# Two-block transformer stack on one core: modulation vectors by wide dot products, with the first block's products set among them

## The reference, cut to what matters

```
mod = silu(c) @ w_ada + b_ada            # c: [1, 2048], w_ada: [2048, 6144]
shift, scale, gate = split(mod, 3)       # 2048 values each
u = rms_norm(x, norm_w) * (1 + scale) + shift
proj = u @ w_in                          # w_in: [2048, 19064], cut into 16 parts
...
x = x + gate * (merged @ w_out)
```

## Time and profile before

| | |
|---|---|
| median of 3 runs | 3606.37 us |
| the profiled execution's own time | 3606.82 us |
| its span, of which all rows tell | 3605.0 us |
| TensorE busy, products | 3485.0 us (97%) |
| TensorE busy, weight loads | 2997.6 us (83%) |
| VectorE busy | 2280.1 us (63%) |
| ScalarE busy | 1689.4 us (47%) |
| GpSimd busy | 31.1 us (1%) |
| moved by DMA | 705.67 MB, mean 196 GB/s |

### The profile page before, as it was taken

The page is one execution under the profiler, slowest core; times in us unless marked ns, Lnnn a source line. Parts: engine busy times, 40 slices in busy tenths (PEclk is TensorE's granted clock), DMA queues, the critical chain, the costliest instruction groups (busy, mean ns, idle before and its releaser), DMA issues. The chain is left out here.

```text
span 3605.0 us, 45068 instructions
## 1 busy us (share of the span) xinstructions
PE 3485.0 (97%) x18836; PEld 2997.6 (83%) x18836; DVE 2280.1 (63%) x2722; ACT 1689.4 (47%) x2076; POOL 31.1 (1%) x61
## 2 busy tenths in 40 slices
PE   7999999998999999999999999999999999999998
PEld 7779878877888887799888888888888789988887
DVE  7687666756677456677655576664566676554544
ACT  2354564454333344545644543433445775443333
POOL 0000000000000000000000000000000000000000
PEclk7899999999999999999999999999999999999999
DMA  9654455456667545444444367765555444455554
GB/s 374 231 203 158 152 199 198 175 185 231 257 253 287 200 181 196 163 161 146 162 144 149 124 223 254 256 258 193 187 187 181 167 166 141 153 211 193 191 186 153
DMA packets 99387, 705.67 MB, mean 196 GB/s; under 512 B 11680, under 2 KB 11696, under 8 KB 15600
## 3 DMA queue, kind: packets, MB, share of 16 engines
q1 hardware_dynamic: 93888, 675.38, 51.5%
q0 software_dynamic: 4864, 24.95, 2.0%
q10 hardware_dynamic: 432, 2.45, 0.2%
HBM read 696.45 MB, written 6.29 MB: 195 GB/s over the span
## 5 line engine op out<-in xcount | busy, mean ns | idle before, releaser
L1365 ACT ACTIVATE HH<-RAW 128x2048 fp32r<-128x2048 f32 x546 | 1045.2, 1914 | 1201.5 <-PE G L1107 905.1
L1701 DVE TENSOR_TENSOR LL<-RAW,HH 128x2048 fp32r<-128x2048 f32 x546 | 1248.0, 2287 | 337.2 <-ACT HH L1365 335.8
L1107 PE MATMUL G<-HH,UH 128*128 128x512 f32 x2560 | 1028.0, 402 | 33.2 <-DVE LL L1701 27.6
L1107 PE MATMUL G<-LL,UH 128*128 128x512 f32 x2560 | 1006.4, 393 | 0.0
L1107 PE MATMUL G<-HH,UL 128*128 128x512 f32 x2560 | 1006.0, 393 | 0.0
L1107 PE MATMUL G<-UH,HH 128*128 128x256 f32 x2080 | 605.0, 291 | 14.5 <-DVE LL L1701 8.4
L1107 PEld LDWEIGHTS G<-HH,UH 128*128 128x128 f32 x2560 | 485.9, 190 | 154.2 <-DVE LL L1701 37.4
L1107 PE MATMUL G<-UL,HH 128*128 128x256 f32 x2080 | 590.5, 284 | 0.0
L1107 PE MATMUL G<-UH,LL 128*128 128x256 f32 x2080 | 590.4, 284 | 0.0
L1107 PEld LDWEIGHTS G<-LL,UH 128*128 128x128 f32 x2560 | 485.6, 190 | 104.9
L1107 PEld LDWEIGHTS G<-HH,UL 128*128 128x128 f32 x2560 | 486.4, 190 | 102.2 <-issue 4.1
(11 more groups left out here) (327 smaller groups left out, 2506.9 us busy)
## 6 DMA issues: line engine op xcount, KB each, us to landing
RAW<-in_w_in_packed_dram SPq DMA_DIRECT2D x402, 1024.0 KB, 4.8
RAW<-in_w_ada_packed_dram SPq DMA_DIRECT2D x96, 1024.0 KB, 5.1
RAW<-in_w_out_packed_dram SPq DMA_DIRECT2D x48, 1024.0 KB, 4.8
RAW<-in_w_o_ssd_packed_dram SPq DMA_DIRECT2D x32, 1024.0 KB, 4.8
RAW<-in_w_o_fox_packed_dram SPq DMA_DIRECT2D x16, 1024.0 KB, 4.8
RAW<-in_w_o_dsa_packed_dram SPq DMA_DIRECT2D x16, 1024.0 KB, 5.2
RAW<-in_w_proj_a_packed_dram SPq DMA_DIRECT2D x16, 1024.0 KB, 4.8
RAW<-in_w_proj_b_packed_dram SPq DMA_DIRECT2D x16, 1024.0 KB, 4.8
```

The lines of the kernel that those rows point to most:

```text
L1107: mm = pe.matmul(to, lt, rh, start=first, stop=end, skip_group_check=True)
L1365: a.activation(HH[g % NH][:, :n], RAW[ch["f"] % NR][:, :n], ACT.Copy).then_inc(*hi_done.up(g))
L1701: v.tensor_tensor(LL[f % NR][:, :n], RAW[f % NR][:, :n], HH[g % NH][:, :n].bitcast(F32), ALU.subtract).then_inc(*lo_done.up(g))
```

## The change

All modulation is done as dot products along the row. The host hands w_ada over transposed (`w_ada_turned`), so that an output column lies on a partition and k runs along the row. c is broadcast over the partitions: `CB` (128x2048, silu of it made once by ScalarE and VectorE) for the opening, `CH` (half of it, loaded by POOL's queue from a copy in DRAM) afterwards. One instruction of VectorE with an accumulator gives 128 columns of the result (`dot`, 128x2048), or in the body two such instructions over 1024 values per chunk (`ada_v`). Results lie in `DOT`, ready as columns; only gate is turned into a row, by four products of 128 columns (`fold_pe`). In the opening eight of 32 dots (two of shift in each group, `ON_PE` = 2) are TensorE's, 16 products of one column each.

The opening (`open`) goes through four groups of four column tiles: eight dots and one chunk of the first block in each, then `am_first` and `u` for that group alone. The products of the chunk of group g stand behind the fourth dot (i = 3) of group g + 1. The ring has eight buffers there (`NX` = 3 more, which lie where YH and YL come later), and five after it. The angle tables, which the opening before contained, go into the slots.

```diff
-NR, NH = 5, 3
+NR, NX, NH = 5, 3, 3
+ON_PE = 2
...
     def fetch(self, src, reader):
-        self.fetches.append({"src": src, "at": (name, self.packed[name] - 1), "reader": reader})
-        return len(self.fetches) - 1
+        f = len(self.fetches)
+        buf = self.ring[self.turn % len(self.ring)]
+        self.turn += 1
+        self.fetches.append({"src": src, "at": (name, self.packed[name] - 1), "reader": reader, "buf": buf,
+                             "before": self.buf_user.get(buf)})
+        self.buf_user[buf] = f
+        return f
...
+    def dot(self, kind, ct, engine):
+        c0 = (D if kind == "scale" else 0) + ct * P
+        src = ("w_ada_turned", 0, c0, P, [(0, D)]) if engine == "dve" else ("w_ada", 0, 0, D, [(c0, P)])
+        token = ("dot_" + engine, kind, ct)
+        self.dots[token[1:]] = self.fetch(src, token)
+        self.put(*token)
+
+    def open(self, block, between, enter):
+        for gi in range(4):
+            dots = [("scale", m, "dve") for m in range(4)] + [("shift", m, "dve") for m in range(4 - ON_PE)]
+            for i, m in zip((0, 3), range(4 - ON_PE, 4)):
+                dots.insert(i, ("shift", m, "pe"))
+            for i, (kind, m, engine) in enumerate(dots):
+                if i == 6:
+                    self.bring(block["chunks"][gi])
+                self.dot(kind, 4 * gi + m, engine)
+                between(gi, i)
+                if gi and i == 3:
+                    self.gemm(block["chunks"][gi - 1])
+            enter(gi)
+            if gi < 3:
+                self.put("lo", block["chunks"][gi]["g"])
+                self.slot()
+        self.pend.append(block["chunks"][3])
+        self.ring, self.turn = sorted(range(NR), key=lambda i: self.buf_user[i]), 0
...
-    def first_x():
-        for t in range(2):
-            put("x_norm", t)
-            yield
-        for c in range(KT // 2):
-            put("x_in", c)
-            yield
+    def first_x(gi, i):
+        if gi == 0 and i == 4:
+            put("x_norm", 0)
+            put("x_norm", 1)
+        if gi == 0 and i == 5:
+            for c in range(KT // 2):
+                put("x_in", c)
...
-    o.ada["list"] = [(0, b, k) for b in range(8) for k in range(4)]
-    for gen in (first_x(), load_layer(0), rope(0), rope(1)):
+    for gen in (load_layer(0), rope(0), rope(1)):
         o.side.add(gen)
-    o.ada_all()
-    while o.side.q:
-        o.slot()
...
     def sync_program(sy):
         for f, e in enumerate(o.fetches):
-            if f >= NR:
-                sy.wait_ge(*reader(f - NR))
+            if e["before"] is not None:
+                sy.wait_ge(*reader(e["before"]))
...
+        def c_half(n):
+            e = o.cb[n]
+            if n == 0:
+                gp.wait_ge(*c_kept.at())
+            if e["last"] is not None:
+                gp.wait_ge(*ada.at(e["last"]))
+            h = e["half"] * D // 2
+            gp.dma_start(CH[:, :], c_dram[0, h:h + D // 2].partition_broadcast(P)).then_inc(*ld_ch.up(n))
...
+        def dot(kind, ct):            # TensorE
+            for k in range(KT):
+                mm = pe.matmul(to, RAW[buf(f)][:, k * P:(k + 1) * P], CT1[:, k:k + 1], start=k == 0, stop=k == KT - 1)
...
+        def fold_pe(l, j):
+            for m in range(4):
+                c = 4 * j + m
+                mm = pe.matmul(BE[:, m * P:(m + 1) * P], GATE[:, c:c + 1].broadcast_to([P, P]), ident, start=True, stop=True)
...
         def u(l, gi):                 # ScalarE
+            if l == 0:
+                for pi in (2 * gi, 2 * gi + 1):
+                    for j in range(2):
+                        i = a.activation(SS[pi % 2][:, j * S:(j + 1) * S], xsT[:, ct, :], ACT.Identity,
+                                         bias=SH[:, ct:ct + 1], scale=AM[:, ct:ct + 1])
...
+        def dot(kind, ct):            # VectorE
+            v.scalar_tensor_tensor(RAW[buf(f)][:, :], RAW[buf(f)][:, :], 0.5, CB[:, :], ALU.mult, ALU.mult,
+                                   accum_out=DOT[:, 0, c:c + 1]).then_inc(*dot_dve.up(kind, ct))
...
+        def ada_v(i):
+            v.wait_ge(*landed(e["f"]))
+            v.wait_ge(*ld_ch.at(e["cb"]))
+            for m in range(2):
+                c = e["part"] * 16 + e["pair"] * 2 + m
+                r = R[:, m * D // 2:(m + 1) * D // 2]
+                done = v.scalar_tensor_tensor(r, r, 0.5, CH[:, :], ALU.mult, ALU.mult, accum_out=DOT[:, e["half"], c:c + 1])
```

More of the change, by code:

```diff
@@ L109, in __init__ @@
         self.packed = {}
+        self.ring, self.turn, self.buf_user = list(range(NR + NX)), 0, {}
         self.fetches = []
@@ L116, in __init__ @@
         self.user = [None, None]
-        self.ada = {"list": [], "i": 0, "job": None, "job2": None, "every": 0, "count": 0, "n": 0, "both": True,
-                    "next": 0, "got": []}
-        self.ada_info, self.folds = [], []
+        self.ada = {"list": [], "i": 0, "job": None, "every": 0, "count": 0, "next": 0, "got": []}
+        self.ada_info, self.cb, self.dots = [], [], {}
     def put(self, *token):
@@ L216, in block, with wblock @@
             ch.update(block=b, first=i == 0, end=i == len(chunks) - 1)
+        return b
+    def block(self, *args, **kw):
+        b = self.begin(*args, **kw)
+        for i, ch in enumerate(b["chunks"]):
             self.push(ch)
-            if i == 1 and soon:
-                self.until(soon()[0])
+            if i == 1 and b["soon"]:
+                self.until(b["soon"]()[0])
         return b
-    def wblock(self, w, c0, evac, ready, kind="cm", x=("U", 0), kts=KT, **kw):
+    def wblock(self, w, c0, evac, ready, kind="cm", x=("U", 0), kts=KT, begun=False, **kw):
         chunks = []
@@ L230, in wblock @@
             chunks.append({"src": src, "w": 512, "nk": 4, "k0": kc * 4, "parts": parts})
-        return self.block(chunks, evac, x, ready, kts, **kw)
+        return (self.begin if begun else self.block)(chunks, evac, x, ready, kts, **kw)
     def ada_fetch(self):
-        l, blk, kc = self.ada["list"][self.ada["next"]]
+        l, part, pair, half = self.ada["list"][self.ada["next"]]
         i = self.ada["next"]
         self.ada["next"] += 1
-        both = self.ada["both"] and kc == 3
-        src = ("w_ada", l, kc * 512, 512, [(blk * 512, 512)])
@@ L252, in ada_chunk @@
[L252 to L266, removed]
-            yield
-        self.put("fold", n)
+        if i == 0:
+            self.c_half(half, None)
@@ L597, in lru @@
         yield
[L601 removed]
     put("start")
[L603 removed]
+    for gen in (load_layer(0), rope(0), rope(1)):
         o.side.add(gen)
[L606 to L612 removed]
+    entered = []
     loaded = [None]
@@ L791, in hybrid_stack @@
         c.__exit__(None, None, None)
+    for tiles, dt in ((RAW, F32), (LL, F32R)):
+        over = []
+        for i in range(NR, NR + NX):
+            c = nc.sbuf_tensor(f"{'RAW' if tiles is RAW else 'LL'}{i}", [P, 2048], dt)
+            over.append(c)
+            tiles.append(c.__enter__())
+        if tiles is RAW:
+            c = nc.sbuf_tensor("CB", [P, D], F32)
+            over.append(c)
+            CB = c.__enter__()
+        for c in reversed(over):
+            c.__exit__(None, None, None)
     YH = sb("YH", [P, KT, S], F32R)
@@ L1114, in begin @@
             pe.wait_ge(*ld_cst.at())
[L1116 to L1120, removed]
-            pe.wait_ge(*c_silu.at())
[L1122 to L1145, removed]
+        def dot(kind, ct):
+            f = o.dots[kind, ct]
+            to = (BD, BE)[ct // 4 % 2][:, ct % 4:ct % 4 + 1]
+            pe.wait_ge(*landed(f))
+            pe.wait_ge(*c_silu.at())
+            if ct >= 8:
+                pe.wait_ge(*am.at(0, ct // 4 - 2))
+            for k in range(KT):
+                mm = pe.matmul(to, RAW[buf(f)][:, k * P:(k + 1) * P], CT1[:, k:k + 1], start=k == 0, stop=k == KT - 1)
+            mm.then_inc(*dot_pe.up(kind, ct))
+        def fold_pe(l, j):
+            pe.wait_ge(*gate_sum.at(l, j))
+            pe.wait_ge(*evac_before("fold", l, j))
+            for m in range(4):
+                c = 4 * j + m
+                mm = pe.matmul(BE[:, m * P:(m + 1) * P], GATE[:, c:c + 1].broadcast_to([P, P]), ident, start=True, stop=True)
+            mm.then_inc(*fold.up(l, j))
         def x_in(c):
```

227 lines of the change are left out of this document (136 added, 91 removed).

## The result

The changed kernel takes 3614.0 us (median of 8 runs, 3610.23 to 3615.15), the kernel before 3605.23 (8 runs, 3600.51 to 3607.97): a ratio of 1.0024, 95% interval 1.0013 to 1.0035. It is 8.8 us slower, the direction of the forecast, and well short of its 3629. The profiled execution took 3610.2 us for a span of 3608.4.

A forecast was written before the change was run, and what follows sets the result against it. TensorE's work was taken to bound the kernel after a start with DMA at a share of 0.99. Opening +32, folds -6.5, waits -4, angle tables +1 summed to +22.5 us: 3629 us, range 3597 to 3652.

The forecast's parts named there:

- step 4: Opening: sc3, the block's chunk, sh0 and sh1 wait for the previous group's block products; groups take 38.5 us, not 23.6.
- The sizes of the opening: Opening: last landing of the first group at 37.3 us, of the fourth at 155.0, products end at 172.6; cost +32 us.
- the tail: Opening, VectorE and ScalarE: from a group's last landing until the block's products could start, 9.3 us.
- Rival A: Opening: shorter chain if the clock is high, groups of 32.3 us, +8 in place of +32, time 3605; chance 0.15.
- Rival B: Opening: the DMA never stops, groups of 23.6 us, opening -15, time 3582; chance 0.1.
- Rival C: Opening and body: the accumulator halves VectorE's rate, a body piece 4.9 us, +30 in place of -4, 3665; chance 0.1.
- VectorE's lighter pieces: Body: 64 modulation pieces 0.6 us shorter each, some 38 us of VectorE; TensorE's waits for low halves -4 us.
- c's halves: Body: loads of 512 KB on POOL's queue land before the next piece needs them, cost 0.
- The angle tables: Moved from the opening into side slots, about 13 us of VectorE, half beside block products: +1 us.
- the sum for the body: After the opening: removed folds -6.5, shorter waits for low halves -4, moved angle tables +1 us.
- a term of 6.5: Body, TensorE: eight removed folds of layer 1's shift and scale, 64 one-column records, -6.5 us.

## Why the prediction was right and wrong, point by point

- **The new wait** (step 4) was right in place and kind, and two runs show it: moving the products 7 us earlier gave 6.9 us a group, giving the block its own buffers gave 44.6 us.
- **The sizes of the opening** held nearly: last landing of the first group 37.3 forecast, 37.8 measured; the tail 9.3, measured 159.64 - 150.50 = 9.1; products of group 0 from 57, measured 55.79; from the first group to the second 40.7, measured 37.9, and then groups of 38.5, measured 37.3 and 37.5; the fourth tail from 155.0, measured 150.5. The opening cost 27.3 us where I had 32. About 2 us are group 0, but not for its first dot: that took 3.63 us and not 7.0 (the clock was high behind the transposes), yet the next dot then waited 4.11 us for its weights and began at 48.94, where I had 50.0; its products took 7.5 us and not 8.3. The rest is about 1 us less in each later group: chunks come every 2.48 us (73.18 to 75.66) and not 2.62, and the products take about 7.9.
- **Rival A** was no more than that one dot, which saved nothing: the others took 6.98 or 6.99 us, and the products of each group began at the low clock.
- **Rival B** couldn't occur in this kernel, but its price was good: for a DMA that never stops it had the first block end at 125.6, and the kernel with two rings has it at 123.33.
- **Rival C** fell. A dot with accumulator has records of 2.289 us and of 0.08 for the read, with two fp32 operands in SBUF, and dots that follow each other start 2.20 us apart (49.79 and 51.99), the read included. I had taken 2.35. The rule of the Trainium skill ("Vector Engine (DVE) Microarchitecture Reference", "Points that are easy to get wrong"), by which I had made it 4.6, is contradicted by these rows, if its half is meant against a plain subtraction of fp32.
- **VectorE's lighter pieces**: I had 38 us less of VectorE's work and -4 of TensorE's waits. The waits of the whole body shrank by 2.0 us, for whatever reason; the run with narrow pieces (+5.3) put back too little to price the term. **c's halves**: VectorE sat idle for 3.1 us ahead of all 128 instructions of L1799, 2.9 of it for their weights; 0 was right. **The angle tables**: no run tried the +1; the stretch behind the opening, in which a part of them fell, cost 1.8 us with everything else in it.
- **The step that failed** is the sum for the body, "- 6.5 - 4 + 1": it counts TensorE's own time of 64 records and its waits for low halves, all priced at one clock, and puts at nothing what a changed order does to the rest, the granted clock above all. The two terms agree with what can be read, which is rough: 6.9 us of the rest, for 6.5, and 2.0 of waits, for 4. What the traces show beside them is about 15 us of the clock in the profiled executions, whose bodies differ by 23.9 us; the medians differ by 18.5. That a changed order alone moves the time by more than the whole sum is shown (+19 for empty steps, +15 and +10 for shifts), and so is the size of folds on TensorE (+20 for a term of 6.5), in which the clock has about 15. The stage of fq, fk and fv says the same: 7.2 us less TensorE busy time, of which three folds at 0.8 us are 2.4, and 3.5 less idle time.
- The sum: opening 27.3 for 32, body -18.5 for -9.5, together +8.8 for +22.5. Two thirds of the miss lie in the body and one third in the opening's sizes, and both err to the same side. The direction was forecast for the right reason.

What stays open: why the changed body keeps the higher clock, and how much of that comes from folds taken out of the evacuation lane (sixteen steps), from lighter pieces or from the new places of the pieces. No run tried one of these by itself in a way that gives the 9 us back: putting folds back costs more than the kernel before paid for them, and shifts of the kernel before cost 11 and 58 us. Nor does the clock simply follow waits: folds on TensorE brought none, and the stretch at 1937 us has none in either kernel.

## What to carry to other kernels

Where loads that are used at once and loads that are held for long share one ring, one late release stops the queue for all; ask of each fetch whose buffer it takes and when that work ends on its own engine's queue. Two small rings cost nothing and were worth 42 us here. In a kernel with a written-out order at 97% on one engine, a removed or added job also moves every later step, so its price is not that of its instructions alone: put a spread on it from runs that change the order alone (here 0 to +19 us, once +58), and split a difference into idle time and time at the low clock before naming a cause.

## What was not expected of the hardware

The accumulator of a VectorE product slows nothing: 2.289 us for 2048 columns, where the plain subtraction of the earlier trace rows takes 2.287, and its read, a record of 0.08 us, adds nothing to the distance of two dots (2.20 us). So a dot product over the free axis costs as much as an elementwise pass. And the granted clock of TensorE is a term of its own in a kernel that keeps this engine busy for 97% of the time: a stretch of 416 products without any wait took 91.1 us at 0.94 in one kernel and 86.5 at 1.00 in the other. These are single executions, and what made the clock fall there is open.
